# Bisecting for the top 256 keys: three score tiles counted on ScalarE in place of two

## The reference, cut to what matters

```
score = einsum('bths,bth->bts', relu(iq . ik), iw) * idx_scale     # per query, all keys
score = where(key <= query, score, -inf)
_, sel = lax.top_k(score, 256)                                      # 256 keys of each query
# softmax attention of the query over the keys in sel alone
```

## Time and profile before

| | us |
|---|---|
| median of three runs | 1716.6 |
| the profiled execution: its own time | 1712.85 |
| its span | 1711.1 |
| busy: TensorE, VectorE, ScalarE, GpSimd | 1546.0, 965.3, 443.5, 551.4 |
| last six rotary units | 205 to 290 |
| S units | 290 to 524 |
| D units | 528 to 670 |

### The profile page before, as it was taken

One profiled execution on the slowest core, in us unless ns is written; L12 is line 12 of the kernel. 1 busy time (PEld: TensorE's weight loads), 2 busy tenths in 40 slices (PEclk: granted clock), 3 DMA queues, 4 the chain that ended last, 5 costly groups with the idle time before them and its releaser, 6 DMA issues.

```text
span 1711.1 us, 20895 instructions
## 1 busy us (share of the span) xinstructions
PE 1546.0 (90%) x7720; PEld 1305.8 (76%) x7720; DVE 965.3 (56%) x1819; ACT 443.5 (26%) x961; POOL 551.4 (32%) x548
## 2 busy tenths in 40 slices
PE   5997884688787999998999999999999999999993
PEld 5885663678686998877888778888888888888882
DVE  5568998799987443277442943333333333333348
ACT  2015334455544764112220111111111111111110
POOL 5341031364462000334333053333333333333100
PEclk9999997788886999999999999999999999999997
DMA  5463043243431102222110041111111111110002
GB/s 214 136 204 129 25 154 129 80 137 130 148 123 46 42 2 87 93 93 74 50 50 1 1 148 49 50 50 50 50 50 49 50 49 50 49 50 25 1 1 98
DMA packets 61332, 128.97 MB, mean 75 GB/s; under 512 B 6960, under 2 KB 34096, under 8 KB 53552
## 3 DMA queue, kind: packets, MB, share of 16 engines
q1 hardware_dynamic: 44208, 100.37, 17.5%
q10 hardware_dynamic: 17024, 27.27, 4.5%
HBM read 100.35 MB, written 27.26 MB: 75 GB/s over the span
## 4 chain that ended last, share of the span: by engine, by line
PE 72%; DVE 19%; issue 4%; ACT 3%; POOL 2%; ACTq 0%; DMA 0%; DVEq 0%; SPq 0%; POOLq 0%
PE banks L584 21%; PE banks L586 21%; PE banks L585 21%; PE banks L741 4%; DVE unread L1245 3%; PE banks L719 2%; DVE score L1216 2%; DVE h_buf L1546 1%; PE banks L751 1%; PE banks L633 1%; DVE bn L1532 1%; PE banks L634 1%; POOL w_lo L575 1%; ACT unread_wide L908 1%; DVE trial L1293 1%
## 5 line engine op out<-in xcount | busy, mean ns | idle before, releaser
L570 POOL TENSOR_SCALAR w_hi<-raw 128x512 fp32r<-128x512 f32 (+1 forms) x272 | 181.4, 693 | 1059.1 <-PE banks L586 770.2
L575 POOL TENSOR_TENSOR w_lo<-raw,w_hi 128x512 fp32r<-128x512 f32 (+1 forms) x272 | 372.5, 1400 | 0.0
L1657 DVE TENSOR_TENSOR h_buf<-h_buf,banks 128x1024 f32<-128x1024 f32 x120 | 146.4, 1220 | 146.6 <-PE banks L586 146.6
L584 PE MATMUL banks<-w_hi,hid_hi 128*128 128x512 f32 x512 | 200.8, 392 | 7.8 <-DVE h_buf L1657 7.8
L584 PE MATMUL banks<-act_hi,w_hi 128*128 128x512 f32 x512 | 200.1, 391 | 1.7 <-DVE act_lo L1525 1.7
L586 PE MATMUL banks<-w_hi,hid_lo 128*128 128x512 f32 x512 | 200.4, 391 | 0.0
L585 PE MATMUL banks<-w_lo,hid_hi 128*128 128x512 f32 x512 | 200.4, 391 | 0.0
L586 PE MATMUL banks<-act_hi,w_lo 128*128 128x512 f32 x512 | 199.9, 390 | 0.0
L585 PE MATMUL banks<-act_lo,w_hi 128*128 128x512 f32 x512 | 199.7, 390 | 0.0
L1621 DVE TENSOR_TENSOR relu_buf<-relu_buf 128x512 f32<-128x512 f32 x64 | 45.8, 716 | 248.3 <-ACT relu_buf L1071 248.3
L1071 ACT ACTIVATE relu_buf<-banks 128x512 f32<-128x512 f32 x64 | 38.3, 598 | 548.9 <-PE banks L586 548.9
(11 more groups left out here) (170 smaller groups left out, 2842.7 us busy)
## 6 DMA issues: line engine op xcount, KB each, us to landing
raw<-w_up_dram SPq DMA_DIRECT2D x16, 1024.0 KB, 4.9
raw<-w_down_dram SPq DMA_DIRECT2D x16, 1024.0 KB, 4.8
q_tile<-qk_dram SPq DMA_DIRECT2D x176, 64.0 KB, 2.1
qk_dram<-q_hi ACTq DMA_DIRECT2D x28, 256.0 KB, 2.1
qk_dram<-roped ACTq DMA_DIRECT2D x28, 256.0 KB, 2.5
x_raw<-x_t_dram SPq DMA_DIRECT2D x8, 512.0 KB, 9.1
raw<-wk_mem_dram SPq DMA_DIRECT2D x4, 1024.0 KB, 5.3
raw<-wv_mem_dram SPq DMA_DIRECT2D x4, 1024.0 KB, 5.1
```

The source lines that it names most:

```text
L570: pool.tensor_scalar(w_hi[s][:, col], raw[c % 2][:, col], 1.0, 1.0, ALU.mult, ALU.mult)\
L575: pool.tensor_tensor(w_lo[s][:, col], raw[c % 2][:, col], w_hi[s][:, col].bitcast(F32), ALU.subtract).then_inc(w_ready, 1)
L584: pe.matmul(dst, lh, rh, start=(first and n == 0), stop=False)
L1657: dve.tensor_tensor(h_buf[:, t, :], h_buf[:, t, :], ring_l[n % 2][:], ALU.add)\
```

## The change

`WIDE` falls from 4 to 3, so column 3 (768 keys) moves from VectorE's narrow columns to ScalarE's wide ones. The groups become `(0, 2)` and `(2, 3)`. The number of wide bits, their places and the budgets stay as they are. The unread results get three places: beside the rotary units in PSUM banks 2 to 7, among the S units in the empty halves of `h_buf` (60, 64 and 68 KB).

```
--- before.py
+++ after.py
@@ -131,7 +131,7 @@
 
 
 N_SEL = NT - FIRST_TOPK_TILE
-WIDE = N_SEL - 2
+WIDE = N_SEL - 3
 TOP_BIT = 30
 SIGN_BIT = -(1 << 31)
 
@@ -262,7 +262,7 @@
         ties = place("ties", [P, N_SEL], F32, 204.3125)
         level = place("level", [P, N_SEL], F32, 204.34375)
         offset = place("offset", [P, N_SEL], F32, 204.375)
-        unread_wide = [place(f"unread_wide{s}", [P, SEQ], BF16, 97 + 4 * s) for s in range(2)]
+        unread_wide = [place(f"unread_wide{s}", [P, SEQ], BF16, 60 + 4 * s) for s in range(3)]
 
         unread = [[place(f"unread{e}_{s}", [P, SEQ], U8, (197, 156)[e] + s) for s in range(2)] for e in range(2)]
         is_tie = unread[1][0]
@@ -308,6 +308,7 @@
         ring_i = [banks[:, s * 2 * HALF:(s + 1) * 2 * HALF] for s in range(4)]
 
         v_bank = [banks[:, s * HALF:(s + 1) * HALF] for s in range(8)]
+        unread_banks = [banks[:, (2 + 2 * s) * HALF:(4 + 2 * s) * HALF] for s in range(3)]
         i_full, i_free = sems("i_full", 4), sems("i_free", 4)
         l_full, l_free = sems("l_full", 2), sems("l_free", 2)
         t_full, t_free = sems("t_full", 2), sems("t_free", 2)
@@ -912,14 +913,14 @@
             def evacuate(r0, r1):
                 for r in range(r0, r1):
                     if wide_bit_beside_rope(2 * r) is not None:
-                        count_wide(wide_bit_beside_rope(2 * r), ring_l)
+                        count_wide(wide_bit_beside_rope(2 * r), unread_banks)
                     for h in range(2):
                         round_roped(r, h)
                         store_roped(r, 0, h)
                     for h in range(2):
                         store_roped(r, 1, h)
                     if wide_bit_beside_rope(2 * r + 1) is not None:
-                        count_wide(wide_bit_beside_rope(2 * r + 1), ring_l)
+                        count_wide(wide_bit_beside_rope(2 * r + 1), unread_banks)
 
             evacuate(0, N_ROPE_FIRST)
             for n in range(len(IDX)):
```

## The result

The changed kernel takes 1727.8 us (median of 4 runs) against 1716.55 for the kernel before (4 runs): 1.0071 times as long, with a 95% interval of 1.0059 to 1.0083. A second set of runs gave 1.0069 (1.0056 to 1.0081). (The ratios given here lie within 0.001 of the quotients of the medians, 1.0065 and 1.0072 for these two.) It is 11 to 12 us slower; 1722.9 was forecast, +6.3, with a range up to 1736. The profiled execution is itself the longest of the four (1728.77, span 1726.9), and the one of before lay under its median, so the two traces differ by 15.8 us of span where the medians differ by 11 to 12.

A forecast was written before the change was run, and what follows sets the result against it. VectorE was taken to bound the stage only in part, the chain of waits hopping between three engines. B 5.4 + C 6.4 + D 1.5 - E 13 + F 6.0 = +6.3 us gave 1722.9 us, range 1709 to 1736.

The forecast's parts named there:

- B: Rotary stage, 205 to 290 us: VectorE waits longer for ScalarE's counts with a third activation, +5.4 us.
- C: S units: twenty counts each 0.95 us longer, 19 us on ScalarE, of which a third shows, +6.4 us.
- D: First 30 S units: passes slightly cheaper, but more tiny steps of a bit in each unit, +1.5 us.
- E: S units from about 31 to 58: VectorE emptied of 33.2 us of passes, -13 us.
- F: Tail, 506 to 541 us: column 3 adds a check pass and a mask on a busy VectorE, +6.0 us.
- The share of the chain: S units: VectorE's passes on the chain of waits for 37 to 40% of their time, used to size its relief.
- Rival 1: S units 31 to 58 held by VectorE alone, so the change is faster: -7.6 us, 1709.0; chance 0.23.
- Rival 2: S units: ScalarE becomes the bound and all 20 longer counts show: +24 us, 1740.5; chance 0.15.
- the wash: Whole kernel: gain and losses cancel to within 3.4 us, 1717; chance 0.16.

The follow-up runs named there:

- e2: Kernel before with a third, unread activation of 768 keys only in ScalarE's 11 counts beside the rotary units: 1.0024 of before, +4.8 us.
- e1: Kernel before with a third, unread activation of 768 keys in all 31 of ScalarE's counts, VectorE's work unchanged: 1.0060 of before, +10.6 us.
- e4: Changed kernel without the mask of column 3 in the tail, its check pass kept: 1.0035 of the kernel before.
- the one-group pair: Changed kernel and kernel before, each with narrow columns in one group, three tiny steps a bit for six: 1.0035 and 0.9962 of before.
- e3: Changed kernel with ScalarE's third activation over 8 keys instead of 768, column 3's threshold taken as 0: 1.0009 of before, +2.4 us.
- f2: Changed kernel with a budget of 0.7 us rather than 1.3 before the 42nd S unit, 1.5 passes a unit: 1.0055 of before.
- f3: Changed kernel with budget 3.0 us behind odd and last rotary halves, and 0.7 in S units before the 38th: 1.0056 of before.
- f4: Kernel before with budgets of 2.5 us behind the last rotary half and 4.0 rather than 1.3 in eight S units: 1.0093 of before.
- the three one-group kernels: One group of narrow columns in the changed kernel (1.0035), the kernel before (0.9962), and the changed kernel with 1.5 passes a unit (1.0037).

## Why the prediction was right, and where a size was off

The sign, the mechanism and each place were right, and the time lay in the range, but the sum was 6.3 for 11 to 12. By its terms, with what measured each (two values: the changed kernel's second profile and its first):

| part | forecast | measured | by |
|---|---|---|---|
| B, rotary stage | +5.4 | +4.8 | e2 |
| C, counts among the S units | +6.4 | +5.8 | e1 less e2 |
| D, first 30 S units, VectorE's side | +1.5 | +2.8, +5.9 | changed less e1 |
| E, emptier VectorE, units 30 to 60 | -13 | -6.6, -8.1 | changed less e1 |
| of it units 30 to 36 | | +3.7, +4.0 | |
| of it units 36 to 60 | | -10.3, -12.2 | |
| F, tail | +6.0 | +5.5 to +5.7 | changed less e1; e4 |

The measured terms add up to 12.4 and 14.0. B, C and F were read from rows and stand within 0.6 us, though the intervals of B and C are wider than that (some 1.5 and 3 us). C had been taken as the share of counts on the chain, a third of 19 us; it came out as 31% (5.8). In the tail, VectorE's work was the time, as its 31.2 of 35 us said.

**The step that was mis-sized is E**, the emptier VectorE, and behind it D. The prediction let 37 to 40% of what leaves VectorE come back, 13 us, from unit 31 on. In units 30 to 60 VectorE is busy 66.5 us in both profiles of the changed kernel, for 104.2 with the load alone, and the stage is 6.6 and 8.1 us shorter: 18 to 22% of 37.7. The relief alone against the kernel before shows 5.5 us. The share of the chain was an average over units in which VectorE was full, and it was spent on a stretch in which, once VectorE had emptied, ScalarE's counts and GpSimd's splits held the chain. That this is why is argued from the chain above; no run separates it.

One edge of E can be placed. The stretch from unit 31 on was taken as relief from its first unit. But at unit 31 the masks of columns 0 to 2 begin, which before came at units 46 to 58. A unit of them is dearer than one of two passes: units 30 to 36 take 25.4 to 25.7 us in the four profiles in which VectorE's order up to there is the changed kernel's, against 21.7 to 22.9 where it is that of before. The prediction moved the masks but charged nothing for it. (Units 46 to 58 were freed of them in turn, so that the two parts of E belong together.)

D counted the tiny steps of the bisection and not what their shift does to others. Two rows of the changed kernel's timeline tell of it, VectorE's and then GpSimd's:

```profile
338.97 3.85 DVE L1493 TENSOR_TENSOR sums<-sums,sink_exp 128x8 f32<-128x8 f32 x1
342.85 0.20 DVE L1494 RECIPROCAL inv_sum<-sums 128x8 f32<-128x8 f32 x1
```

```profile
335.44 2.40 POOL L571 TENSOR_SCALAR w_hi<-raw 128x512 fp32r<-128x512 f32 x4
337.77 5.03 POOL L576 TENSOR_TENSOR w_lo<-raw,w_hi 128x512 fp32r<-128x512 f32 x4
```

An addition of eight elements, 0.16 us at the median, takes 3.85 and ends at 342.82, with the last of GpSimd's four splits (342.80). The changed kernel's two profiles, the relief alone and the thin one have it alike (3.85 us, begun 1.2 us into the four splits); in the other ten kernels the longest such step takes 0.7 to 1.4. Between units 9 and 12, where it stands, the changed kernel loses 2.4 us to before and the relief alone does too, while the load alone loses nothing. It is a collision in time that the trace of before could not have placed, and it isn't even certain: without the mask of column 3 the same step began as early in the splits and was let in after 1.36 us. The Trainium skill has the rule ("SBUF — State Buffer", "Who interferes with whom"): an operation with two SBUF inputs that comes second waits until GpSimd's instruction is over. The trace agrees and is harsher, since it waited for the three behind it as well.

A second such collision tells the changed kernel's two profiles apart. It is a step of a bit (L1294) in unit 24, begun 1.8 us into four splits in both; the first profile and then the second:

```profile
391.48 4.95 POOL L576 TENSOR_TENSOR w_lo<-raw,w_hi 128x512 fp32r<-128x512 f32 x4
393.23 3.21 DVE L1294 TENSOR_TENSOR trial<-refused,trial_next 128x1 int32<-128x1 int32 x1
```

```profile
390.76 4.96 POOL L576 TENSOR_TENSOR w_lo<-raw,w_hi 128x512 fp32r<-128x512 f32 x4
392.52 0.77 DVE L1294 TENSOR_TENSOR trial<-refused,trial_next 128x1 int32<-128x1 int32 x1
```

Once it is held to the end of the fourth split, once let in 2.4 us sooner, and the first 30 units differ by 3.1 us. So D less the 2.4 us of the first collision is 0.4 us in the second profile, and 3.5 in the first, of which the second collision explains 2.4. What is left of D is 0.4 and 1.1 us, under the 1.5 forecast, and the rest is collisions. That the denser steps explain it was my theory, and the one-group pair speaks against it.

Rival 1 (the occupied engine is the bound) fell: with its 33 us taken off, and a third of the load put on ScalarE, the kernel was not faster (e3). The rule to relieve the most occupied engine first (the Trainium skill, "Perfetto Trace Analysis", "Identifying Performance Opportunities") points at VectorE, at 91%, and relief of it did show here (E, and the one-group pair), but its worth was far from its size; the chain's share (37 to 40%) came nearer and was still twice too high. Rival 2 (all 20 counts show) fell with e1, and the wash with the measurement.

## What to carry to other kernels

Three engines that hand each other small pieces within two units of lead form a ring in which none is the bound, and work moved from the fullest (91%) to a much emptier one (52%) can lose: here 29 us more of ScalarE's activations cost 10.6 us, and 33 us off VectorE brought none, as what units 30 to 60 gained (5.5 us there) went again in the tail (5.8). A line's share of the chain of waits sized the load rightly (6.4 us for 5.8) and the relief at about twice what came (13 for 6.6 to 8.1), since it holds for the stretch as it is and not for one from which a third of the work is gone. And look where in time the relief falls and what moves up into its place; when the moved work has tiny steps, cutting their number (6.1 us for three steps less a bit) was worth more than moving the passes.

## What the runs showed of the hardware

Beside four GpSimd splits back to back (some 1.25 us each), a VectorE addition of 128x8 begun 1.2 us into them lasted 3.85 us, to the end of the fourth, in four profiles of five, and 1.36 us in the fifth. Begun 1.1 us into them, in the three one-group kernels, it lasted 0.20 to 0.21. In the kernel before, that step never took more than 1.12 us. Other short steps with two inputs were held to the end of the fourth too: 3.21 us in one profile of the changed kernel, and 4.87 us, begun within 0.2 us of the start of the first split, in f2, f3 and f4. TensorE's granted clock in the S units was 0.81 and 0.87 in the two stretches before, and 0.80 and 0.95 after, the last where its waits for VectorE (4.3 us) had gone; no run separates what raised it.
